# Run-in of a two-layer decoder kernel: one interleaved rounding order for the first weight parts and x pieces of both tiles

## The chip, the cores and the metric

The kernel runs on one core of a Trainium2 chip. The metric is the device time of one execution in microseconds; less is better. Before the change it is 1027.71 us, the median of three runs (1027.68 to 1027.79).

## What is computed

A residual stream x of 256 tokens by 1024 channels passes two layers, each a half-step SwiGLU FFN, a mixer (sliding-window attention in layer 0, gated DeltaNet in layer 1) and a second half-step FFN, then a last RMS norm. All is float32. The change is in the first FFN's first products alone:

```
def rms_norm(x, w):
    y = xf * lax.rsqrt(jnp.mean(xf * xf, axis=-1, keepdims=True) + NORM_EPS)
    return (y * w).astype(x.dtype)

def swiglu_ffn(h, w_gate_up, w_down):
    gate, up = jnp.split(h @ w_gate_up, 2, axis=-1)
    return (jax.nn.silu(gate) * up) @ w_down

h = h + 0.5 * swiglu_ffn(rms_norm(h, ffn1_norm[layer]), ffn1_w_gate_up[layer], ffn1_w_down[layer])
```

## The kernel before

**Products.** Every float32 operand is cut into two parts that TensorE takes at full rate: a high part (rounded by ScalarE, a Copy into fp32r) and a low part (the operand less its high part, by VectorE). `products` (L1691) then makes three matmuls of one: high by high, high by low, low by high. The x side is 128 tokens (a tile t of two), the weight side 512 columns.

**Weights.** Weights stream through a ring of four buffers of 128x2048, one "unit" each (w_raw, w_hi, w_lo). Unit u of the first FFN holds four 128-row slices (parts j = 0 to 3 of 512 columns) of one half kh of the 1024 input channels: units 0 and 1 are the first chunk's two halves, 2 and 3 the second chunk's, and so on. Units 0 to 2 are loaded, rounded and waited for by parts (`first_part` L508 on SP, `parts_hi` L732 on ScalarE, `parts_lo` L1153 on VectorE); from unit 3 on a unit is rounded whole (`split_hi` L725, `split_lo` L1147).

**x.** x is transposed by TensorE (`enter`, L1704) in quarters: a quarter n is a tile t and a half of the channels, four 128x128 transposes (pieces) into PSUM, in the order (t, half) = (0,0), (1,0), (0,1), (1,1). ScalarE evacuates each piece with the norm weight as scale into xT_hi (`enter_hi` L756), VectorE makes xT_lo from the same PSUM piece (`enter_lo` L1191). The factor of the RMS norm (rstd) is applied to results later. It needs squares of the whole x on ScalarE (`square` L749), then a root.

**The run-in.** SP issues the loads in order of use (from L557: x quarter, two weight parts, x quarter, two parts, x quarter, two parts of unit 1, x quarter, the rest; unit 2's parts; then unit 3 and on). ScalarE issues three small loads of norm weights and one of the convolution's weights (48 KB, L852), which is first used by a transpose at L1818, behind the first chunk. TensorE makes 14 warm-up transposes (L1835), the transpose of the norm rows (L1840), the first quarter of x and six more warm-ups. Then ScalarE (L858) and VectorE (L1329) take for each j one x piece of the first quarter and one weight part of unit 0, in turns, and only then the second and third quarters, unit 1's parts, the fourth quarter and unit 2's parts:

```
            for j in range(4):
                act.activation(xT_hi[:, j, 0:P], bank[FIRST_BANKS[j]][:, 0:P], ACT.Copy,
...
                act.wait_ge(part_loaded[0][j], 16)
...
                act.activation(w_hi[0][:, at], w_raw[0][:, at], ACT.Copy).then_inc(first_hi if j < 3 else hi_ready, 1)
            ffn(0)
```

TensorE's first chunk is `in_unit` (L1717), called for kh = 0 and 1: for tile 0 the four groups (one `products` call each) of parts 0 to 3, then for tile 1 the same. While kh = 0 and t = 0 it puts the remaining quarters' transposes behind groups 0, 2 and 3. So 16 groups, 48 matmuls:

```
                        if e == 0 and kh == 0 and t == 0 and j != 1:
                            enter(e, max(j, 1))
```

**Behind it.** The convolution transpose (L1818), then chunk 1 (`gate_chunk`, units 2 and 3; L1763 and L1765). Behind unit 2 stand `first_transposes` (L1771): the rstd rows and the transposes of the first chunk's result h. ScalarE meanwhile takes the squares, unit 3, the root, the silu of the first chunk (each of the last two behind a table load), units 4 and 5, and the high part of h; VectorE follows with the low parts (L1219, L1150, and L1227 for h). Chunk 2 on TensorE waits for h's low part (hT_lo_ready). All engines run their queues in order; every wait is a semaphore count.

## Time and profile before

| | |
|---|---|
| median of three runs | 1027.71 us (1027.68 to 1027.79) |
| profiled execution | 1027.81 us, its span 1026.1 us |
| TensorE busy (matmul) | 1015.8 us, 99% of the span |
| VectorE busy | 675.1 us, 66% |
| ScalarE busy | 569.1 us, 55% |
| GpSimd busy | 59.7 us, 6% |
| first product starts | 7.92 us |
| convolution transpose (first chunk done) | 20.65 us |

The span runs from the first to the last instruction of the profiled execution; starts are counted from its beginning. In the rows PE is TensorE's matmul, PEld its weight load, DVE VectorE, ACT ScalarE, SPq and ACTq the DMA issues of SP and ScalarE, and L and a number a line of the kernel. A row of the timeline can merge equal instructions that follow each other (x4): its second number is then the time from the first's start to the last's end. A matmul's duration includes its passage through the array, so matmuls overlap and their spacing is read from their starts.

### The profile page before, as it was taken

What the parts mean: (1) busy time and instruction counts of PE and PEld (TensorE: products, weight loads), DVE (VectorE), ACT (ScalarE), POOL (GpSimd) and SP (SyncE); (2) the same over time, 40 slices, a digit from 0 to 9 for tenths busy, and PEclk for the clock granted to TensorE, in tenths of its full rate; (3) what the DMA queues carried; (4) which work ended last, traced back from release to release, by engine and by line L of the source; (5) the groups of instructions that cost most, each with busy time, mean ns of one, the idle gap of its engine ahead of it and who ended that gap; (6) DMA issues with size and microseconds to landing.
All of it is one profiled execution on the core that took longest, in us unless ns stands there. A gap on an engine that the chain in (4) does not pass through costs nothing.

```text
span 1026.1 us, 15442 instructions
## 1 busy us (share of the span) xinstructions
PE 1015.8 (99%) x5784; PEld 880.5 (86%) x5784; DVE 675.1 (66%) x1005; ACT 569.1 (55%) x907; POOL 59.7 (6%) x120
## 2 busy tenths in 40 slices
PE   9999999999999999999999999999999999999997
PEld 7888888887888888888888888999999988888886
DVE  5766765576566776635766764688597666776733
ACT  7645543457465554536545543578567655554532
POOL 0000000110000000000000000404205100000000
PEclk9999999999999999999999999999999999999999
DMA  9665466343346555663666466343242347556521
GB/s 323 218 211 194 167 242 205 134 165 111 98 131 227 172 189 209 217 199 100 197 212 195 166 244 205 114 161 124 83 145 83 124 144 234 176 176 218 215 87 42
DMA packets 124308, 175.81 MB, mean 171 GB/s; under 512 B 7360, under 2 KB 97760, under 8 KB 124256
## 3 DMA queue, kind: packets, MB, share of 16 engines
q1 hardware_dynamic: 121552, 172.77, 50.6%
q10 hardware_dynamic: 2704, 2.33, 0.7%
q8 instruction: 34, 0.56, 0.2%
q14 instruction: 18, 0.15, 0.0%
HBM read 174.02 MB, written 1.06 MB: 171 GB/s over the span
## 4 chain that ended last, share of the span: by engine, by line
PE 97%; DVE 1%; ACT 1%; issue 0%; POOL 0%; ACTq 0%; POOLq 0%; DVEq 0%
PE bank L1763 29%; PE bank L1693 15%; PE bank L1695 15%; PE bank L1694 14%; PE bank L1765 14%; PE bank L2087 2%; PE bank L2081 2%; PE bank L1990 1%; PE bank L1714 1%; PE bank L1925 1%; PE bank L1956 1%; PE bank L1855 1%; PE bank L2187 0%; DVE x_sb L1187 0%; PE bank L1835 0%
## 5 line engine op out<-in xcount | busy, mean ns | idle before, releaser
L1763 PE MATMUL bank<-xT,w_hi 128*128 128x512 f32 x1280 | 444.9, 394 | 0.0
L1150 DVE TENSOR_TENSOR w_lo<-w_raw,w_hi 128x2048 fp32r<-128x2048 f32 x152 | 347.1, 2288 | 105.6 <-ACT w_hi L730 105.0
L730 ACT ACTIVATE w_hi<-w_raw 128x2048 fp32r<-128x2048 f32 x153 | 294.0, 1929 | 118.1 <-PE bank L1695 118.1
L1765 PE MATMUL bank<-xT,w_lo 128*128 128x256 f32 x1280 | 354.8, 277 | 0.0
L1763 PEld LDWEIGHTS bank<-xT,w_hi 128*128 128x128 f32 x1280 | 240.0, 188 | 55.9
L1765 PEld LDWEIGHTS bank<-xT,w_lo 128*128 128x128 f32 x1280 | 240.3, 188 | 0.1
L1693 PE MATMUL bank<-w_hi,hT_hi 128*128 128x512 f32 x352 | 137.5, 391 | 0.0
L1695 PE MATMUL bank<-w_hi,hT_lo 128*128 128x512 f32 x352 | 137.1, 389 | 0.0
L1694 PE MATMUL bank<-w_lo,hT_hi 128*128 128x512 f32 x352 | 137.0, 389 | 0.0
L796 ACT ACTIVATE silu_g<-bank 128x256 f32<-128x256 f32 x80 | 26.3, 382 | 175.4 <-PE bank L1765 175.4
L1237 DVE TENSOR_TENSOR silu_g<-bank,silu_g 128x256 f32<-128x256 f32 x80 | 30.2, 419 | 119.6 <-ACT silu_g L796 119.6
L1695 PEld LDWEIGHTS bank<-w_hi,hT_lo 128*128 128x128 f32 x352 | 66.1, 188 | 13.7
L1693 PEld LDWEIGHTS bank<-w_hi,hT_hi 128*128 128x128 f32 x352 | 66.1, 188 | 13.5
L1694 PEld LDWEIGHTS bank<-w_lo,hT_hi 128*128 128x128 f32 x352 | 66.1, 188 | 13.4
L1693 PE MATMUL bank<-w_hi,xT 128*128 128x512 f32 x144 | 59.9, 416 | 1.1 <-DVE w_lo L1343 0.7
L1695 PE MATMUL bank<-w_hi,xT 128*128 128x512 f32 x144 | 56.4, 392 | 0.0
L1694 PE MATMUL bank<-w_lo,xT 128*128 128x512 f32 x144 | 56.2, 390 | 0.0
L1693 PE MATMUL bank<-xT,w_hi 128*128 128x256 f32 x192 | 56.0, 292 | 0.0
L1695 PE MATMUL bank<-xT,w_lo 128*128 128x256 f32 x192 | 54.3, 283 | 0.0
L1694 PE MATMUL bank<-xT,w_hi 128*128 128x256 f32 x192 | 54.3, 283 | 0.0
L763 ACT ACTIVATE xT<-bank,norm_cols 128x128 fp32r<-128x128 f32 x92 | 26.2, 369 | 36.0 <-PE bank L1714 36.0
L1200 DVE SCALAR_TENSOR_TENSOR xT<-bank,norm_cols,xT 128x128 fp32r<-128x128 f32 x92 | 25.6, 343 | 24.6 <-ACT xT L763 24.6
(310 smaller groups left out, 1214.0 us busy)
## 6 DMA issues: line engine op xcount, KB each, us to landing
w_raw<-in_ffn_w_gate_up SPq DMA_DIRECT2D x170, 512.0 KB, 4.7
w_raw<-in_ffn_w_down SPq DMA_DIRECT2D x88, 512.0 KB, 4.2
w_raw<-in_gdn_w_in SPq DMA_DIRECT2D x32, 512.0 KB, 4.4
w_raw<-in_attn_w_in SPq DMA_DIRECT2D x12, 512.0 KB, 4.3
w_raw<-in_attn_w_out SPq DMA_DIRECT2D x8, 512.0 KB, 4.0
w_raw<-in_gdn_w_out SPq DMA_DIRECT2D x8, 512.0 KB, 3.9
w_raw<-in_ffn_w_gate_up SPq DMA_DIRECT2D x12, 256.0 KB, 5.5
x_sb<-in_x SPq DMA_DIRECT2D x4, 256.0 KB, 5.0
```

The costliest lines, as they stand in the source:

```text
L730: act.activation(w_hi[u0 % RING][:], w_raw[u0 % RING][:], ACT.Copy).then_inc(hi_ready, 1)
L763: z = act.activation(xT_hi[:, kt, t * P:(t + 1) * P], enter_bank(e, n, j), ACT.Copy, scale=norm_cols[:, norm_col(e, kt):norm_col(e, kt) + 1])
L796: z = act.activation(to[:, m, :], banks[2 * k + m][:, SEQ:2 * SEQ], ACT.Copy)
L1150: dve.tensor_tensor(w_lo[u0 % RING][:], w_raw[u0 % RING][:], w_hi[u0 % RING][:].bitcast(F32), ALU.subtract).then_inc(split_ready, 1)
L1200: z = dve.scalar_tensor_tensor(xT_lo[:, kt, t * P:(t + 1) * P], enter_bank(e, n, j), norm_cols[:, norm_col(e, kt):norm_col(e, kt) + 1], xT ...
L1237: z = dve.tensor_tensor(g[:, m, :], banks[m][:, 0:SEQ], g[:, m, :], ALU.add)
L1693: pe.matmul(out_ap, a[0], b[0], start=start, stop=False, **kw)
L1694: pe.matmul(out_ap, a[0], b[1], start=False, stop=False, **kw)
L1695: return pe.matmul(out_ap, a[1], b[0], start=False, stop=stop, **kw)
L1763: pe.matmul(banks[m][:], w[0], xT[:, kt, :, :].rearrange("p s n -> p (s n)"), start=(kt == 0), stop=False, skip_group_check=True)
L1765: z = pe.matmul(banks[m][:, 0:SEQ], w[1], xT_hi[:, kt, :], start=False, stop=(kt == KT - 1), skip_group_check=True)
L2081: z = pe.matmul(bank[b][:, h * P:(h + 1) * P], a(h), m(h), start=True, stop=True)
```

## The change

A list PIECES gives one order for the 12 operands of unit 0: four weight parts and the x pieces of both tiles' first halves. ScalarE and VectorE both follow it. Every x piece of the first two quarters has a bank or part of a bank of its own; quarter 2 goes to bank 1. The low part of every piece but three counts up first_split, for which TensorE waits by piece (PIECE_COUNT). TensorE's first chunk is the new `first_units`: in each unit the groups come in the order (t, j) = (0,0), (0,1), (1,0), (1,1), (0,2), (1,2), (0,3), (1,3), with the transposes of the other quarters behind the first, fifth and eighth group of unit 0. ScalarE and VectorE take the third quarter, two parts of unit 1, the fourth quarter, two parts, unit 2. The convolution rows' load goes from ScalarE's queue to SP's, behind unit 2's parts. The first FFN's `first_transposes` move from behind unit 2 to before the third part of unit 3. The first x quarter is transposed ahead of the norm rows, with 9 warm-ups before and 8 behind (14 and 6 before), in bank 6 instead of 5.

```diff
--- before.py
+++ after.py
@@ -276,7 +276,10 @@
             X_of = [[X[t], Lm[t]] for t in range(TT)]
 
         bank = [ctx.enter_context(nc.psum_tensor(f"bank{i}", [P, BANK], F32)) for i in range(8)]
-        FIRST_BANKS = [4, 0, 1, 3]
+        FIRST_BANKS = [[4, 0, 1, 5], [6, 7, 4, 0]]
+        PIECES = [("w", 0), (0, 0), (0, 1), ("w", 1), (0, 2), (1, 0), (1, 1), ("w", 2), (0, 3), (1, 2), ("w", 3), (1, 3)]
+        LAST_PIECES = [(0, 3), ("w", 3), (1, 3)]
+        PIECE_COUNT = {piece: 1 + n for n, piece in enumerate([q for q in PIECES if q not in LAST_PIECES])}
 
 
         ENTER_BANKS = {0: (4, 6), 1: (4, 2), 2: (4, 2), 3: (4, 6), 5: (4, 2)}
@@ -293,8 +296,10 @@
             t, half = quarters(e)[n]
             if e == E_GDN:
                 return bank[((4, 5), (6, 0), (4, 4), (5, 5))[n][j // 2]][:, j * P:(j + 1) * P]
-            if e == 0 and n == 0:
-                return bank[FIRST_BANKS[j]][:, 0:P]
+            if e == 0 and n < 2:
+                return bank[FIRST_BANKS[n][j]][:, 0:P]
+            if e == 0 and n == 2:
+                return bank[1][:, j * P:(j + 1) * P]
             return bank[ENTER_BANKS[e][t] + half][:, j * P:(j + 1) * P]
 
         def chunk_banks(f, j):
@@ -568,6 +573,7 @@
             first_part(1, 3)
             for j in range(4):
                 first_part(2, j)
+            sp.dma_start(conv_rows, gdn_conv_w[0].rearrange("j (t p) -> (j t) p", p=P)).then_inc(conv_loaded, 16)
             ffn(0, ffn1_w_gate_up[0], ffn1_w_down[0])
             for n, col in enumerate(ATT_COLS):
                 for kh in range(2):
@@ -729,9 +735,9 @@
                     act.wait_ge(unit_done, u0 - RING + 1 + 4 * i)
                 act.activation(w_hi[u0 % RING][:], w_raw[u0 % RING][:], ACT.Copy).then_inc(hi_ready, 1)
 
-            def parts_hi(u0):
-
-                for j in range(4):
+            def parts_hi(u0, js=range(4)):
+
+                for j in js:
                     act.wait_ge(part_loaded[u0][j], 16)
                     at = slice(j * BANK, (j + 1) * BANK)
                     act.activation(w_hi[u0][:, at], w_raw[u0][:, at], ACT.Copy).then_inc(
@@ -807,9 +813,10 @@
                 e, u = E_FFN[f], U_FFN[f]
                 if f == 0:
 
-                    enter_hi(e, range(1, 3))
-                    parts_hi(1)
+                    enter_hi(e, range(2, 3))
+                    parts_hi(1, range(2))
                     enter_hi(e, range(3, 4))
+                    parts_hi(1, range(2, 4))
                     parts_hi(2)
                 else:
                     enter_hi(e)
@@ -849,19 +856,22 @@
             for n, w in enumerate([ffn1_norm, mix_norm, ffn2_norm]):
                 act.dma_start(norm_rows[n * 2 * KT:(n + 1) * 2 * KT, :],
                               w.rearrange("l (t p) -> (l t) p", p=P)).then_inc(rows_loaded, 16)
-            act.dma_start(conv_rows,
-                          gdn_conv_w[0].rearrange("j (t p) -> (j t) p", p=P)).then_inc(conv_loaded, 16)
-            act.wait_ge(cols_psum, 1)
-            act.activation(norm_cols[:], bank[7][:, 0:NORM_ROWS], ACT.Copy).then_inc(cols_ready, 1)
-            act.wait_ge(cols_ready, 1)
-            act.wait_ge(xT_psum, 1)
-            for j in range(4):
-                act.activation(xT_hi[:, j, 0:P], bank[FIRST_BANKS[j]][:, 0:P], ACT.Copy,
-                               scale=norm_cols[:, norm_col(0, j):norm_col(0, j) + 1]).then_inc(
-                                   first_hi if j < 3 else xT_hi_ready, 1)
-                act.wait_ge(part_loaded[0][j], 16)
-                at = slice(j * BANK, (j + 1) * BANK)
-                act.activation(w_hi[0][:, at], w_raw[0][:, at], ACT.Copy).then_inc(first_hi if j < 3 else hi_ready, 1)
+            for piece in PIECES:
+                tile, j = piece
+                if tile == "w":
+                    act.wait_ge(part_loaded[0][j], 16)
+                    at = slice(j * BANK, (j + 1) * BANK)
+                    act.activation(w_hi[0][:, at], w_raw[0][:, at], ACT.Copy).then_inc(
+                        hi_ready if piece in LAST_PIECES else first_hi, 1)
+                else:
+                    act.wait_ge(xT_psum, tile + 1)
+                    act.activation(xT_hi[:, j, tile * P:(tile + 1) * P], enter_bank(0, tile, j), ACT.Copy,
+                                   scale=norm_cols[:, norm_col(0, j):norm_col(0, j) + 1]).then_inc(
+                                       xT_hi_ready if piece in LAST_PIECES else first_hi, 1)
+                if piece == ("w", 0):
+                    act.wait_ge(cols_psum, 1)
+                    act.activation(norm_cols[:], bank[7][:, 0:NORM_ROWS], ACT.Copy).then_inc(cols_ready, 1)
+                    act.wait_ge(cols_ready, 1)
             ffn(0)
 
 
@@ -1150,9 +1160,9 @@
                 dve.tensor_tensor(w_lo[u0 % RING][:], w_raw[u0 % RING][:], w_hi[u0 % RING][:].bitcast(F32),
                                   ALU.subtract).then_inc(split_ready, 1)
 
-            def parts_lo(u0):
-
-                for j in range(4):
+            def parts_lo(u0, js=range(4)):
+
+                for j in js:
                     at = slice(j * BANK, (j + 1) * BANK)
                     if j < 3:
                         dve.wait_ge(part_hi, 3 * (u0 - 1) + j + 1)
@@ -1277,10 +1287,10 @@
                     enter_lo(e, 3)
                     split_lo(PHASE_UNIT[e] + 2)
                 else:
-                    enter_lo(e, 1)
                     enter_lo(e, 2)
-                    parts_lo(1)
+                    parts_lo(1, range(2))
                     enter_lo(e, 3)
+                    parts_lo(1, range(2, 4))
                     parts_lo(2)
                 inverse_rms(TT * (e + 1))
 
@@ -1325,23 +1335,25 @@
                 after(dve.tensor_scalar(ang[:, 1], ang[:, 1], TWO_PI / 4, None, ALU.add))
                 dve.tensor_scalar(ang[:], ang[:], PI_BELOW, -PI_BELOW, ALU.min, ALU.max).then_inc(angle_ready, 1)
 
-            dve.wait_ge(cols_ready, 1)
-            for j in range(4):
-                at = slice(j * BANK, (j + 1) * BANK)
-                if j < 3:
-                    dve.wait_ge(first_hi, 2 * j + 1)
+            for piece in PIECES:
+                tile, j = piece
+                if piece in PIECE_COUNT:
+                    dve.wait_ge(first_hi, PIECE_COUNT[piece])
+                if tile == "w":
+                    if piece in LAST_PIECES:
+                        dve.wait_ge(hi_ready, 1)
+                    at = slice(j * BANK, (j + 1) * BANK)
+                    dve.tensor_tensor(w_lo[0][:, at], w_raw[0][:, at], w_hi[0][:, at].bitcast(F32),
+                                      ALU.subtract).then_inc(split_ready if piece in LAST_PIECES else first_split, 1)
                 else:
-                    dve.wait_ge(xT_hi_ready, 1)
-                z = dve.scalar_tensor_tensor(xT_lo[:, j, 0:P], bank[FIRST_BANKS[j]][:, 0:P],
+                    if piece in LAST_PIECES:
+                        dve.wait_ge(xT_hi_ready, tile + 1)
+                    dve.wait_ge(cols_ready, 1)
+                    at = slice(tile * P, (tile + 1) * P)
+                    dve.scalar_tensor_tensor(xT_lo[:, j, at], enter_bank(0, tile, j),
                                              norm_cols[:, norm_col(0, j):norm_col(0, j) + 1],
-                                             xT_hi[:, j, 0:P].bitcast(F32), ALU.mult, ALU.subtract)
-                if j < 3:
-                    dve.wait_ge(first_hi, 2 * j + 2)
-                else:
-                    z.then_inc(xT_lo_ready, 1)
-                    dve.wait_ge(hi_ready, 1)
-                dve.tensor_tensor(w_lo[0][:, at], w_raw[0][:, at], w_hi[0][:, at].bitcast(F32),
-                                  ALU.subtract).then_inc(first_split if j < 3 else split_ready, 1)
+                                             xT_hi[:, j, at].bitcast(F32), ALU.mult, ALU.subtract).then_inc(
+                                                 xT_lo_ready if piece in LAST_PIECES else first_split, 1)
             ffn(0, None)
 
 
@@ -1714,27 +1726,49 @@
                     z = pe.transpose(enter_bank(e, n, j), x_sb[:, t, kt * P:(kt + 1) * P], ident[:])
                 z.then_inc(xT_psum, 1)
 
+            def first_units(banks):
+
+                def tile_part(kh, t, j):
+                    return products(bank[banks[t]][:], x_of(4 * kh + j, t), ring(kh, slice(j * BANK, (j + 1) * BANK)),
+                                    start=(kh == 0 and j == 0), stop=(kh == 1 and j == 3))
+
+                for n, (t, j) in enumerate([(0, 0), (0, 1), (1, 0), (1, 1), (0, 2), (1, 2), (0, 3), (1, 3)]):
+                    for piece in ((t, j), ("w", j)):
+                        if piece in PIECE_COUNT:
+                            pe.wait_ge(first_split, PIECE_COUNT[piece])
+                        elif piece == ("w", 3):
+                            wait_split(pe, 0)
+                        else:
+                            pe.wait_ge(xT_lo_ready, t + 1)
+                    z = tile_part(0, t, j)
+                    if n == 0:
+                        pe.wait_ge(first_split, PIECE_COUNT[0, 1])
+                        enter(0, 1)
+                    elif n == 4:
+                        pe.wait_ge(first_split, PIECE_COUNT[0, 2])
+                        enter(0, 2)
+                    elif n == 7:
+                        z.then_inc(unit_done, 1)
+                        enter(0, 3)
+                for t, j in [(0, 0), (0, 1), (1, 0), (1, 1), (0, 2), (1, 2), (0, 3), (1, 3)]:
+                    pe.wait_ge(xT_lo_ready, 2 + t + 1)
+                    if j < 3:
+                        pe.wait_ge(part_split, j + 1)
+                    else:
+                        wait_split(pe, 1)
+                    z = tile_part(1, t, j)
+                z.then_inc(unit_done, 1)
+
             def in_unit(u0, i, kh, banks, e=None):
 
 
-                by_parts = u0 < FIRST and not looped(i)
-                if not by_parts:
-                    wait_split(pe, u0, i)
-                for t in range(TT):
-                    if e is not None and (e or kh or t):
+                wait_split(pe, u0, i)
+                for t in range(TT):
+                    if e is not None:
                         pe.wait_ge(xT_lo_ready, 4 * e + quarters(e).index((t, kh)) + 1)
                     for j in range(4):
-                        if by_parts and t == 0:
-                            if j < 3 and u0 == 0:
-                                pe.wait_ge(first_split, j + 1)
-                            elif j < 3:
-                                pe.wait_ge(part_split, 3 * (u0 - 1) + j + 1)
-                            else:
-                                wait_split(pe, u0)
                         z = products(bank[banks[t]][:], x_of(4 * kh + j, t), ring(u0, slice(j * BANK, (j + 1) * BANK)),
                                      start=(kh == 0 and j == 0), stop=(kh == 1 and j == 3))
-                        if e == 0 and kh == 0 and t == 0 and j != 1:
-                            enter(e, max(j, 1))
                     if t == TT - 1:
                         z.then_inc(unit_done, 1)
                     if e and kh == 0:
@@ -1753,6 +1787,8 @@
                     if not by_parts:
                         wait_split(pe, u0, i)
                     for q in range(4):
+                        if f == 0 and j == 1 and kh == 1 and q == 2 and not looped(i):
+                            first_transposes(f)
                         if by_parts and q < 3:
                             pe.wait_ge(part_split, 3 * (u0 - 1) + q + 1)
                         elif by_parts:
@@ -1765,7 +1801,7 @@
                             z = pe.matmul(banks[m][:, 0:SEQ], w[1], xT_hi[:, kt, :], start=False,
                                           stop=(kt == KT - 1), skip_group_check=True)
                     z.then_inc(unit_done, 1)
-                    if j == 1 and kh == 0 and not looped(i):
+                    if f and j == 1 and kh == 0 and not looped(i):
                         first_transposes(f)
 
             def first_transposes(f):
@@ -1811,8 +1847,11 @@
                 return hT_hi[:, at], hT_lo[:, at]
 
             def ffn(f, e_next):
-                for kh in range(2):
-                    in_unit(U_FFN[f] + kh, 0, kh, FIRST_CHUNK[f], E_FFN[f])
+                if f == 0:
+                    first_units(FIRST_CHUNK[f])
+                else:
+                    for kh in range(2):
+                        in_unit(U_FFN[f] + kh, 0, kh, FIRST_CHUNK[f], E_FFN[f])
                 if f == 0:
                     pe.wait_ge(conv_loaded, 16)
                     pe.transpose(bank[5][:, 0:CONV_ROWS], conv_rows,
@@ -1832,14 +1871,14 @@
             def warm(count):
 
                 for n in range(count):
-                    pe.transpose(bank[5][:, 0:P], ident[:], ident[:])
+                    pe.transpose(bank[6][:, 0:P], ident[:], ident[:])
 
             pe.wait_ge(ident_ready, 1)
-            warm(14)
+            warm(9)
+            enter(0, 0)
             pe.wait_ge(rows_loaded, 16 * 3)
             pe.transpose(bank[7][:, 0:NORM_ROWS], norm_rows, ident[0:NORM_ROWS, 0:NORM_ROWS]).then_inc(cols_psum, 1)
-            enter(0, 0)
-            warm(6)
+            warm(8)
             ffn(0, E_ATT)
 
 
```

## Rows read from the trace of the kernel before

**Rows 1.** The page: the chain that ended last, share of the span by engine.
```profile
PE 97%; DVE 1%; ACT 1%; issue 0%; POOL 0%; ACTq 0%; POOLq 0%; DVEq 0%
```

**Rows 2.** Timeline of TensorE (PE), first 21 us.
```profile
start us, us, engine line op out<-in xcount [idle before <-releaser]
1.60 3.25 PE L1835 MATMUL bank<-ident 128*128 128x128 f32 x14 [1.60 <-POOL ident L607]
...
5.95 1.26 PE L1835 MATMUL bank<-ident 128*128 128x128 f32 x6
...
7.92 0.50 PE L1693 MATMUL bank<-w_hi,xT 128*128 128x512 f32 x1 [0.71 <-DVE w_lo L1343]
...
8.73 0.60 PE L1714 MATMUL bank<-ident,x_sb 128*128 128x128 f32 x4
...
9.08 0.48 PE L1693 MATMUL bank<-w_hi,xT 128*128 128x512 f32 x1
...
11.96 0.65 PE L1714 MATMUL bank<-ident,x_sb 128*128 128x128 f32 x4
...
15.21 0.39 PE L1693 MATMUL bank<-w_hi,xT 128*128 128x512 f32 x1
...
20.65 0.25 PE L1818 MATMUL bank<-ident,h_row 96*128 96x96 f32 x1
```

**Rows 3.** Timeline of ScalarE (ACT) and VectorE (DVE), 6 to 18 us.
```profile
6.26 0.37 ACT L859 ACTIVATE xT<-bank,norm_cols 128x128 fp32r<-128x128 f32 x1 [0.90 <-PE bank L1714]
...
6.53 0.62 ACT L864 ACTIVATE w_hi<-w_raw 128x512 fp32r<-128x512 f32 x1
...
7.04 0.36 ACT L859 ACTIVATE xT<-bank,norm_cols 128x128 fp32r<-128x128 f32 x1
...
7.18 0.69 DVE L1343 TENSOR_TENSOR w_lo<-w_raw,w_hi 128x512 fp32r<-128x512 f32 x1
...
7.79 0.35 DVE L1335 SCALAR_TENSOR_TENSOR xT<-bank,norm_cols,xT 128x128 fp32r<-128x128 f32 x1
...
8.57 0.63 ACT L864 ACTIVATE w_hi<-w_raw 128x512 fp32r<-128x512 f32 x1 [0.40 <-DMA w_raw<-in_ffn_w_gate_up]
...
11.43 1.14 ACT L763 ACTIVATE xT<-bank,norm_cols 128x128 fp32r<-128x128 f32 x4 [0.42 <-PE bank L1714]
...
12.60 1.12 DVE L1200 SCALAR_TENSOR_TENSOR xT<-bank,norm_cols,xT 128x128 fp32r<-128x128 f32 x4 [0.43 <-ACT xT L763]
...
17.61 1.09 ACT L750 ACTIVATE y_sb<-x_sb 128x1024 f32<-128x1024 f32 x1
```

**Rows 4.** Timeline of SP's issues, and what the norm rows' landing released.
```profile
0.82 0.40 SPq L544 DMA_DIRECT2D x_sb<-in_x  x1
...
1.27 1.31 SPq L511 DMA_DIRECT2D w_raw<-in_ffn_w_gate_up  x2
...
4.77 0.18 PEld L1840 LDWEIGHTS bank<-ident,h_row 48*128 48x128 f32 x1 [0.33 <-DMA h_row<-in_ffn_norm]
```

**Rows 5.** DMA view of single issues (x at 0.82; parts 0, 1): KB, us to landing.
```profile
x_sb<-in_x SPq DMA_DIRECT2D x1, 256.0 KB, 2.9
...
w_raw<-in_ffn_w_gate_up SPq DMA_DIRECT2D x1, 256.0 KB, 3.9
...
w_raw<-in_ffn_w_gate_up SPq DMA_DIRECT2D x1, 256.0 KB, 4.6
```

**Rows 6.** Timeline behind the run-in, 19 to 33 us.
```profile
19.69 1.94 ACT L730 ACTIVATE w_hi<-w_raw 128x2048 fp32r<-128x2048 f32 x1
...
27.13 4.49 DVE L1150 TENSOR_TENSOR w_lo<-w_raw,w_hi 128x2048 fp32r<-128x2048 f32 x2 [1.33 <-ACT w_hi L730]
...
31.55 0.68 DVE L1227 TENSOR_TENSOR hT_lo<-bank,hT_hi 128x512 fp32r<-128x512 f32 x1
...
32.62 0.39 PE L1763 MATMUL bank<-xT,w_hi 128*128 128x512 f32 x1
```

**Rows 7.** Warm-up transposes by line: ns min/median/max, first and last start us.
```profile
L1835 PE MATMUL bank<-ident x20: 273/421/473, 1.6 to 6.9; 128*128 128x128 f32 x20
```

**Rows 8.** Windows, 0 to 7 us: busy us of each engine, PEclk behind POOL.
```profile
core 0: us, PE busy (x) PEld busy (x) DVE busy (x) ACT busy (x) POOL busy (x), PEclk, DMA share, GB/s
0.00:7.00 7.00, 5.40 (x25) 4.96 (x25) 0.26 (x1) 2.23 (x4) 0.70 (x6) 1.00 0.63 184
```

## Prediction

> **What bounds the kernel now.** The page first: the chain that ended last is 97% TensorE [rows 1], so the time is the length of TensorE's work plus the few places where it waits. The timeline of the first 45 us, TensorE's rows alone, shows those places in the run-in [rows 2]: 14 warm-up transposes from 1.60, six more from 5.95 to 7.2, then nothing until the first product at 7.92, released by VectorE's first weight part. The first FFN chunk is 16 groups of three products (48 matmuls) with 12 transposes of x between them, and it ends at 20.65, where the convolution transpose starts. The prices of TensorE's steps come from these rows: a group that follows a wait lasts 8.73 - 7.92 = 0.81 us, a group in a steady stream (20.65 - 15.21) / 8 = 0.68, four transposes delay the next group by 9.08 - 8.73 = 0.35 and their result is whole after 0.60. Without any wait the 16 groups and 12 transposes would take 16 x 0.68 + 0.13 + 3 x 0.35 = 12.06 us; they take 20.65 - 7.92 = 12.73. From 15.21 on, where unit 1 begins, TensorE never waits. So what can be won is the start at 7.92 and about 0.6 us of gaps, and whatever the new order loses counts in full, because everything behind 20.65 is TensorE's chain.
>
> The rows of ScalarE and VectorE [rows 3] give the other prices. ScalarE: a weight part (128x512) is 0.62 long and the next operation starts 7.04 - 6.53 = 0.51 later; an x piece (128x128) is 0.36 and the next starts 0.27 later. VectorE: a part 0.69, next after 7.79 - 7.18 = 0.61; an x piece 0.34, next after (1.12 - 0.34) / 3 = 0.26. An operation released by the other engine starts about 0.04 behind its end; TensorE starts 0.05 behind VectorE (7.18 + 0.69 to 7.92). Arrivals [rows 4, 5]: the first x quarter lands at 0.82 + 2.9 = 3.72, the first weight part at 1.27 + 3.9 = 5.17, the second, whose issue ends the 1.31 us from 1.27 and so begins near 2.0, at 2.0 + 4.6 = 6.6, the norm rows by 4.77; the third part landed at 8.57 [rows 3], the last x quarter at 11.96 [rows 2].
>
> **The change, step by step.** *Start.* 9 warm-ups at the pace of the six (1.26 / 6 = 0.21) end near 3.5; the x quarter follows at its landing, 3.75, and is whole by 4.9; norm rows and 8 warm-ups follow, done near 6.7. ScalarE now rounds part 0 first, 5.20 to 5.82, then copies the norm columns (5.72), then x piece 0 at 5.99 to 6.36, x piece 1 at 6.26, part 1 at its landing, 6.60 to 7.22. VectorE: part 0 at 5.86, x piece 0 at 6.47 to 6.82, x piece 1 to 7.08, part 1 at 7.26 to 7.95. First product: 6.82 + 0.05 = 6.87, against 7.92: 1.05 us won.
>
> *Unit 0.* Group (0,0) ends 7.68; the four transposes of tile 1 are whole at 8.28; group (0,1) meanwhile, to about 8.8. Group (1,0) needs the first of those pieces through ScalarE (8.32 to 8.68) and VectorE (8.72 to 9.07): it starts at 9.12, a wait of 0.3. It ends 9.93, (1,1) 10.61, (0,2) 11.29: part 2 (landed 8.57, ScalarE 8.86, VectorE 9.52 to 10.21) is ready. Transposes of the third quarter at 11.29, whole at 11.89. The last three groups have their operands (VectorE's last piece ends near 11.6) and end at 11.64 + 2.14 = 13.78; the fourth quarter's transposes end unit 0 at 14.13. Before, TensorE was at this point at 15.21: it is now 1.08 ahead.
>
> *Unit 1* gives it back. ScalarE and VectorE have run out of work by 11.6 and wait for the third quarter: ScalarE 11.93 to 13.07 (four pieces, 1.14), VectorE 13.11 to 14.23, and only then does VectorE take weight part 0 of unit 1, ready at 14.84. TensorE waits from 14.13 to 14.89 and restarts: that group lasts 0.81. Group (0,1) ends 16.38. Group (1,0) needs the fourth quarter: transposes whole at 14.38, ScalarE (after two parts, idle from 14.0) 14.42 to 15.56, VectorE 15.60 to 16.72. TensorE starts it at 16.77, a wait of 0.39, and goes on with 0.81 + 5 x 0.68: the chunk ends at 20.98. Before, tile 1's groups of unit 0 stood between these operands and their use; now they have been spent. Sum to here: +0.33.
>
> *Behind it.* ScalarE's squares started at 17.61; now its queue holds four x pieces and six parts from 14.42: 14.42 + 1.0 + 6 x 0.52 = 18.54, later by 0.93. That lateness runs on through table loads, first chunk and splits of units 4 and 5 to VectorE, which follows ScalarE there (idle 1.33 before the two L1150) and reaches the low part of h at 31.55 [rows 6]. TensorE needs it at 32.62 for chunk 2: slack 32.62 - 32.23 = 0.39. TensorE is 0.33 later, VectorE 0.93: 33.16 + 0.05 against 32.95 is a wait of 0.26, with the restart some 0.35. The first transposes of h, moved from behind unit 2 into the middle of unit 3 (some 2.8 us of products later), cost the same wherever they stand, and give h's rows, which come from the late first chunk, more time; their result finds VectorE still at its two splits, so the move costs nothing at 31.55 and saves nothing there. Sum: 0.33 + 0.35 = +0.68.
>
> *Edits costed at nothing.* Three warm-ups fewer, and another bank for them: TensorE idles before the first product in any case. Banks of their own for pieces: no wait is added beyond those counted. The extra waits on TensorE, ScalarE and VectorE are met when reached, save the ones above; if each took some hundredths the sum would grow by up to 0.2. The convolution rows' load moves from ScalarE's queue (fourth there, beside the first parts) behind 16 transfers on SP. It puts one issue of 0.6 us ahead of unit 3's loads, which ScalarE needed only at 19.69 [rows 6] and now needs 0.93 later; the rows themselves are needed at 20.98, nearly ten us after their issue (16 transfers at 1.31 / 2 from 0.82), against landing times of 2.9 to 4.6 [rows 5]. In its old place it took bytes beside part 1, which lands 6.6 - 5.17 = 1.43 behind part 0: 48 KB against 256 KB are at most 48/256 of that, 0.27, and at least nothing. The sum above passes little of it on, since it hangs on TensorE's own transposes; I take -0.08, nearer to nothing, and the forecast is +0.6. The Trainium skill (DMA: Bandwidth & Descriptors, section "Issuing engines are not separate DMA queues") says that transfers issued by different engines interleave on the same 16 DMA engines. By that rule the load costs the same bytes wherever it is issued, and only its place in time can help; if that place is worth nothing, the sum stays +0.68 instead of +0.60. Part 1's late landing fits the rule without proving it.
>
> The profiled execution took 1027.81 us around a span of 1026.1, the median of three is 1027.71; I put the 0.6 on the median: 1028.3.
>
> **Rivals.** *A: the lead is kept.* If unit 1's operands came in time, the end would move by -1.05 to -1.3 (the old gaps too), half of it if only one of the two waits comes: 1026.5 to 1027.6. For: VectorE's work for 16 pieces and 8 parts is 16 x 0.26 + 8 x 0.61 = 9.0 us in a stretch of 14. Against: each quarter goes through three engines whole, 0.60 + 1.14 + 1.12 us before the first use, and its transposes stand later in the groups' order than before. Chance 0.22.
>
> *B: slower by over 0.2%, the array's pace.* The granted clock is recorded as 1.00 over the first 7 us [rows 8], but transposes come every 0.21 us from 5.95 (1.26 / 6) and every 0.11 at 8.73 ((0.60 - 0.27) / 3): the early ones go at the pace of the lower level, 1.2 GHz, the later ones at 2.4, and the shortest warm-up (273 ns, median 421) is already one of the faster kind, after almost unbroken work since 1.60 [rows 7]. The first product would now stand at 6.87, just there, behind three fewer warm-ups and two gaps of some 0.2. If the pace rose only after another stretch as long as the first (1.60 to 6.9, 5.3 us), half of that, 2.6, would be lost, some 0.2 of it in the wait at 9.12: 1028.3 + 2.4 = 1030.7. It decides from 1.5 us lost. The Trainium skill (TensorE: Matmul & The Clock Gate, Part 1) has the throttled state as the default that activity releases, and warns that recorded clock events can be unreliable; the pace of these rows agrees with both. Chance 0.05.
>
> *C: the early start fails.* If norm rows or part 0 come late behind the new order, or piece 0 of x (third in ScalarE's queue now) waits, the first product stays near 7.9 and the waits of unit 1 remain, since they hang on TensorE's own transposes: +0.6 + 1.0, 1029.3. Chance 0.06.
>
> **Numbers.** Forecast case 0.67 (+0.0 to +1.1: no lateness at chunk 2, or every added wait and both restarts dearer), A 0.22, B 0.05, C 0.06. The range runs from half of A to the top of the forecast case: 1027.1 to 1029.0, leaving out the lower half of A, B and C, 0.2 together. What a measurement can tell here is 0.2%, 2.06 us; all but B lie inside. Faster 0.02, same 0.93, slower 0.05.
>
> **What would show it.** Right: first product at 6.8 to 7.0 and at full pace (second one 0.34 behind the first), a gap near 9, waits before the first and third group of unit 1, convolution transpose near 21.0, squares near 18.5, a wait before chunk 2's first product. Wrong: no gap at 14 to 15 and the convolution transpose at 19.9 or earlier (A), matmuls 0.43 apart (512 columns at 1.2 GHz) behind the first product (B), first product after 7.5 (C).

## The result, and the profile after

The changed kernel takes 1030.12 us (median of 20, 1028.62 to 1032.00), the kernel before 1027.74 beside it (20, 1027.41 to 1029.74). The medians are 2.4 us apart (slower), where +0.6 was forecast; the ratio on record is 1.0021, 95% interval 1.0014 to 1.0027. The ratios given here are those on record, not quotients of the medians (1.0023 here), so they can differ from them in the fourth place. The executions fall in groups: six at 1028.62 to 1028.95, five at 1029.86 to 1030.14, six at 1030.48 to 1030.81, three at 1031.90 to 1032.00. The profiled one took 1030.54. The lines of the page for it:

```profile
span 1028.8 us, 15460 instructions
...
PE 1017.2 (99%) x5781; PEld 880.0 (86%) x5781; DVE 675.3 (66%) x1005; ACT 569.3 (55%) x907; POOL 59.8 (6%) x120
...
PE 95%; ACT 2%; DVE 2%; issue 1%; DMA 0%; SPq 0%; ACTq 0%; DVEq 0%
```

The last line answers to [rows 1]. TensorE lost two points of the chain to the others: followed in time, the chain now lies on ScalarE and VectorE from 14.56 to chunk 2's first product at 33.35 (x pieces, weight parts, squares, root and silu, the splits, the low part of h). The timeline of the changed kernel shows where (start, length, instruction, idle before it and its releaser):

```profile
7.00 0.50 PE L1705 MATMUL bank<-w_hi,xT 128*128 128x512 f32 x1 [0.90 <-DVE xT L1353]
...
9.24 0.50 PE L1705 MATMUL bank<-w_hi,xT 128*128 128x512 f32 x1
...
15.10 0.47 PE L1705 MATMUL bank<-w_hi,xT 128*128 128x512 f32 x1 [0.57 <-DVE w_lo L1171]
...
16.92 0.50 PE L1705 MATMUL bank<-w_hi,xT 128*128 128x512 f32 x1 [0.20 <-DVE xT L1210]
...
18.70 1.06 ACT L756 ACTIVATE y_sb<-x_sb 128x1024 f32<-128x1024 f32 x1
...
21.14 0.25 PE L1857 MATMUL bank<-ident,h_row 96*128 96x96 f32 x1
...
32.62 0.68 DVE L1237 TENSOR_TENSOR hT_lo<-bank,hT_hi 128x512 fp32r<-128x512 f32 x1
...
33.35 0.50 PE L1799 MATMUL bank<-xT,w_hi 128*128 128x512 f32 x1
```

Against [rows 2, 3, 6]: first product 7.92 to 7.00, convolution transpose 20.65 to 21.14, squares 17.61 to 18.70, h's low part 31.55 to 32.62, chunk 2's first product 32.62 to 33.35. So the changed kernel is 0.73 late at chunk 2's first product. At 134 us, where the first FFN's gate and up part ends, it is 2.73 late, and 2.7 at the end. The other 2.0 us arise between 33 and 134 us, where no engine's order was touched and TensorE shows no wait. The windows of TensorE alone, 40 to 100 us (us, busy and matmuls in brackets, granted clock, DMA share, GB/s), first the kernel before, then the changed one:

```profile
40.00:100.00 60.00, 60.00 (x348) 1.00 0.63 201
```
```profile
40.00:100.00 60.00, 60.00 (x341) 1.00 0.59 190
```

Both are 100% busy at a clock of 1.00, with the same instructions. One starts 348 matmuls, the other 341. The work of a unit is 16 pairs, each one matmul of 512 columns and one of 256. Start by start, a unit takes 5.547 us before and 5.65 to 5.66 after, in every unit from chunk 2 to the end of the first FFN's gate and up part. The spacings form a pattern that repeats: over two pairs in 0.693 us in the first rhythm, over three pairs in 1.060 us in the second. These are called the fast and the slow rhythm below. The stretch of 18 units costs 18 x 0.106 = 1.9 us, and 0.1 is the restart behind the wait at 33.35. The other three FFNs run in the fast rhythm behind chunk 2 in both profiles.

Where did the slow rhythm begin in this profile? Not at the wait. Six pairs take 28.88 - 26.80 = 2.08 us ahead of h's transposes, and 32.70 - 30.58 = 2.12 behind them, still ahead of the wait:

```profile
26.80 0.39 PE L1799 MATMUL bank<-xT,w_hi 128*128 128x512 f32 x1
...
28.88 0.39 PE L1799 MATMUL bank<-xT,w_hi 128*128 128x512 f32 x1
...
29.80 0.60 PE L1818 MATMUL bank<-ident,h_row 128*128 128x128 f32 x4
...
30.58 0.40 PE L1799 MATMUL bank<-xT,w_hi 128*128 128x512 f32 x1
...
32.70 0.40 PE L1799 MATMUL bank<-xT,w_hi 128*128 128x512 f32 x1
```

So there are two candidates, h's transposes and the wait ahead of chunk 2. The experiments take them apart.

### The profile page after: what moved, and what is told of

Same layout as the page of the kernel before. It is cut to its first block, busy times and chain, and to the rows that moved or that the text cites. A ratio compares the mean times of both kernels' runs of the same rounds, so it can differ in the third digit from the quotient of the medians.

```text
span 1028.8 us, 15460 instructions
## 1 busy us (share of the span) xinstructions
PE 1017.2 (99%) x5781; PEld 880.0 (86%) x5781; DVE 675.3 (66%) x1005; ACT 569.3 (55%) x907; POOL 59.8 (6%) x120
## 4 chain that ended last, share of the span: by engine, by line
PE 95%; ACT 2%; DVE 2%; issue 1%; DMA 0%; SPq 0%; ACTq 0%; DVEq 0%
PE bank L1799 28%; PE bank L1705 14%; PE bank L1707 14%; PE bank L1706 14%; PE bank L1801 14%; PE bank L2126 2%; PE bank L2120 2%; PE bank L2029 1%; PE bank L1726 1%; PE bank L1964 1%; PE bank L1995 1%; PE bank L1894 1%; DVE w_lo L1160 0%; DVE x_sb L1197 0%; PE bank L2226 0%
## 5 line engine op out<-in xcount | busy, mean ns | idle before, releaser
L809 ACT ACTIVATE hT_hi<-h_row 128x512 f32 (+1 forms) x40 | 25.3, 633 | 29.0 <-DVE h_row L1259 29.0
```

The lines of the kernel that those rows point to most:

```text
L809: act.activation(hT_hi[:, bass.ds((j + 2 * i) * BANK, BANK)], h_row[j % 2][:].rearrange("p m n -> p (m n)"), ACT.Copy).then_inc(hT_hi_read ...
```

## Experiments: what changes the rhythm

The experiments ran in four groups, each on one chip beside the kernel before; "of n" counts executions. The kernel before had 33, 32, 27 and 21 executions in the four groups, medians 1027.79, 1027.69, 1027.74, 1027.73, and 11 of these 113 above 1029.2.

**h's transposes back in their place**, in the changed kernel:

```diff
-                        if f == 0 and j == 1 and kh == 1 and q == 2 and not looped(i):
-                            first_transposes(f)
...
-                    if f and j == 1 and kh == 0 and not looped(i):
+                    if j == 1 and kh == 0 and not looped(i):
                         first_transposes(f)
```

> The changed kernel with one part undone: the transposes of the first chunk's h stand behind unit 2 again instead of in the middle of unit 3. Theory 1 (two rhythms: the 512/256-column pairs of the first FFN run at 5.55 or 5.65 us per unit of 16 pairs, and the transposes' place decides which one the following 18 units take): units from unit 3 on at 5.547, chunk 2 starts 0.6 to 0.8 behind the kernel before, the time 1028.3 to 1028.8. Rival (the late run-in, its shifted loads or its wait ahead of chunk 2 slow the units): units stay at 5.65 and the time near 1030.3. In both the wait for h's rows behind unit 2 is under 0.2 us.

Median 1030.44 (of 11), ratio 1.0023 (1.0014 to 1.0032); four executions at 1028.2 to 1028.65, five at 1030.4 to 1030.8, two above 1032. The profiled one (1028.53) has all 18 units at 5.547. The place doesn't decide alone, and neither does the late run-in by itself: one kernel runs both ways.

**That move alone, in the kernel before**: the same lines the other way round.

> The kernel before with this part of the change alone: the transposes of h moved from behind unit 2 into the middle of unit 3. Theory 1 (the place decides the rhythm): the units behind it at 5.65 and the time near 1029.7, though the run-in is the old one. Rival (the run-in's lateness slows the units): units at 5.547 and 1027.7, as before.

Median 1027.85, ratio 0.9999 (0.9990 to 1.0008); three of 11 above 1029.3. The move by itself costs nothing in most executions. Its profile caught one of the three (1030.35): units at 5.65, and the early products 0.36 to 0.59 apart until 9.7 us. (Here and with the transposes cut in two, further down, the move in the kernel before has six of 22 executions above 1029.2, the kernel before 11 of 113. Whether the move makes late executions more frequent can't be told from so few.)

**Quarters of x transposed earlier**, in the changed kernel:

```diff
-                    elif n == 4:
+                    elif n == 3:
                         pe.wait_ge(first_split, PIECE_COUNT[0, 2])
                         enter(0, 2)
+                    elif n == 5:
+                        enter(0, 3)
                     elif n == 7:
                         z.then_inc(unit_done, 1)
-                        enter(0, 3)
```

> The changed kernel with the third quarter's transposes of x behind the fourth group of unit 0 instead of the fifth, and the fourth quarter's behind the sixth instead of the eighth. By the account of the run-in (quarters reach ScalarE too late) the waits at unit 1's first and third group fall from 0.57 and 0.20 idle to under 0.25 each, and the convolution transpose starts at 20.1 to 20.3 instead of 21.14; ScalarE's squares start near 17.6 instead of 18.70. If the waits hang on something else (arrivals, weight parts) it stays at 20.9 or later. The time is then the one that the rhythm gives: 1027.3 in the fast one, 1029.3 in the slow one.

> Both edits: quarters' transposes earlier and h's transposes behind unit 2 again. Convolution transpose at 20.1 to 20.3; behind unit 2 h's rows are waited for by up to 0.6 us, since TensorE is there 0.5 earlier than in the kernel before. If the place decides the rhythm: units at 5.547 and 1027.3 to 1027.8, at or below the kernel before; if not, up to 1029.5.

The timeline of the first one:

```profile
17.47 1.09 ACT L756 ACTIVATE y_sb<-x_sb 128x1024 f32<-128x1024 f32 x1
...
20.10 0.25 PE L1858 MATMUL bank<-ident,h_row 96*128 96x96 f32 x1
```

The convolution transpose moves from 21.14 to 20.10 and the squares from 18.70 to 17.47, and TensorE's waits at unit 1's first and third group are gone from the profile: the account of unit 1's waits is right. Of the 1.04 us, 0.25 is an earlier first product (6.75, not 7.00) and 0.79 a shorter chunk. The time doesn't follow: 1029.39 (ratio 1.0012, 1.0003 to 1.0021), one execution at 1027.42 and ten at 1029.2 to 1029.7. With h's transposes back in their place it is 1029.60 (1.0020, 1.0011 to 1.0029), none below 1029.0 and four of 11 at 1031.0 to 1031.3; 1029.5 at most was expected if the place doesn't decide. Both profiles show a tiny wait ahead of chunk 2 (0.02 to 0.04 us beyond the usual spacing of the pairs), the fast rhythm ahead of it and the slow one behind it. That suggested the next four.

**The wait ahead of chunk 2 taken away, added, and the changed kernel again.** Taken away (in the changed kernel, and in the one with earlier quarters):

```diff
                 split_lo(u + 4)
-                split_lo(u + 5)
+                if f:
+                    split_lo(u + 5)
...
                                   ALU.subtract).then_inc(hT_lo_ready, 1)
+                if f == 0:
+                    split_lo(U_FFN[f] + 5)
                 dve.wait_ge(rows_ready, ROWS_FFN[f])
```

Added, in the kernel before:

```diff
             def first_hT_lo(f):
 
+                if f == 0:
+                    dve.tensor_scalar(y_sb[:, 0, :], x_sb[:, 0, :], 1.0, None, ALU.mult)
                 dve.wait_ge(hT_hi_ready, NCH * f + 1)
```

> The changed kernel with the wait ahead of chunk 2 taken away: VectorE makes h's low part before unit 5's instead of behind it. Theory (a wait right ahead of chunk 2's first product picks the rhythm of all the pairs behind it anew in every execution; without one they keep the rhythm they have, mostly the fast one): no idle ahead of chunk 2, most executions in the fast rhythm, median near 1028.3. Rival 1 (the rhythm is drawn somewhere in the run-in, or by the place of h's transposes): the time falls only by the wait itself, 0.35, and most executions stay slow, median near 1030.

> The kernel before with such a wait added: one extra VectorE operation over 128x1024 ahead of h's low part, some 0.6 to 1.1 us, against 0.34 of slack. Its result goes to a scratch tile. Theory: the wait itself costs 0.3 to 0.9 and most executions change to the slow rhythm, median 1029.5 to 1030.7. Rival (the rhythm is drawn elsewhere): the wait alone, 1028.1 to 1028.7.

> Earlier quarters' transposes of x and no wait ahead of chunk 2. Theory: the fast rhythm in most executions and the run-in's gain kept, median 1027.0 to 1027.4, below the kernel before. Rival: 1029.2.

> The changed kernel unaltered, beside the first one on the same chip. Theory: executions fall in groups near 1028.7, 1030.0 to 1030.8 and 1032, most of them in the middle one; its profile, whichever group it falls in, has units 4 to 21 of the first FFN all at 5.547 or all at 5.65 us.

The changed kernel again: 1030.53 (of 10), one at 1028.72, nine at 1030.3 to 1030.8. Its timeline at the wait, the pairs' first matmuls alone:

```profile
31.51 0.39 PE L1799 MATMUL bank<-xT,w_hi 128*128 128x512 f32 x1
...
31.86 0.39 PE L1799 MATMUL bank<-xT,w_hi 128*128 128x512 f32 x1
...
32.20 0.39 PE L1799 MATMUL bank<-xT,w_hi 128*128 128x512 f32 x1
...
32.55 0.39 PE L1799 MATMUL bank<-xT,w_hi 128*128 128x512 f32 x1
...
32.90 0.39 PE L1799 MATMUL bank<-xT,w_hi 128*128 128x512 f32 x1
...
33.42 0.19 PEld L1799 LDWEIGHTS bank<-xT,w_hi 128*128 128x128 f32 x1 [0.33 <-DVE hT_lo L1237]
...
33.88 0.40 PE L1799 MATMUL bank<-xT,w_hi 128*128 128x512 f32 x1
...
34.24 0.40 PE L1799 MATMUL bank<-xT,w_hi 128*128 128x512 f32 x1
...
34.59 0.40 PE L1799 MATMUL bank<-xT,w_hi 128*128 128x512 f32 x1
...
34.94 0.40 PE L1799 MATMUL bank<-xT,w_hi 128*128 128x512 f32 x1
...
35.30 0.40 PE L1799 MATMUL bank<-xT,w_hi 128*128 128x512 f32 x1
```

Four pairs take 32.90 - 31.51 = 1.39 us ahead of the wait and 35.30 - 33.88 = 1.42 behind it; from the unrounded starts, a unit's worth is 5.55 and 5.65. Here the rhythm changes at the wait. In the first profile of the same kernel it had changed at h's transposes.

The wait added to the kernel before shows as 0.16 us at TensorE's weight load, and at its matmul as hardly anything. The pair's start comes 0.35 behind the one ahead of it, as usual, and only the next comes late, at 0.46 instead of 0.35:

```profile
31.27 0.69 DVE L1227 TENSOR_SCALAR y_sb<-x_sb 128x1024 f32<-128x1024 f32 x1
...
31.87 0.68 DVE L1229 TENSOR_TENSOR hT_lo<-bank,hT_hi 128x512 fp32r<-128x512 f32 x1
...
32.26 0.39 PE L1765 MATMUL bank<-xT,w_hi 128*128 128x512 f32 x1
...
32.61 0.19 PEld L1765 LDWEIGHTS bank<-xT,w_hi 128*128 128x128 f32 x1 [0.16 <-DVE hT_lo L1229]
...
32.61 0.50 PE L1765 MATMUL bank<-xT,w_hi 128*128 128x512 f32 x1
...
33.07 0.40 PE L1765 MATMUL bank<-xT,w_hi 128*128 128x512 f32 x1
```

The median rose to 1029.67 (ratio 1.0013, 1.0004 to 1.0022): four executions at 1027.5 to 1028.15, seven at 1029.4 to 1029.9, while of the kernel before's 32 beside it five are above 1029.2. A wait whose own cost is some 0.1 costs 2 us in seven executions of 11. Its profile (1029.77) goes from 5.547 ahead of the wait to 5.65 behind it.

Taken away from the changed kernel, the median is 1029.50 (1.0014, 1.0005 to 1.0023): five executions at 1027.8 to 1028.5, three at 1029.5 to 1029.7, three at 1030.1 to 1030.4. That lies between the two theories. The profiled execution has no wait for h and keeps 5.547 from unit 3's last two parts to the end of the stretch:

```profile
31.25 0.69 DVE L1238 TENSOR_TENSOR hT_lo<-bank,hT_hi 128x512 fp32r<-128x512 f32 x1 [0.74 <-ACT hT_hi L792]
...
31.86 2.28 DVE L1160 TENSOR_TENSOR w_lo<-w_raw,w_hi 128x2048 fp32r<-128x2048 f32 x1
```

With earlier quarters as well it is 1027.42 (0.9998, 0.9989 to 1.0007), seven of 11 at 1026.97 to 1027.47 and four near 1029. A wait is a cause of the rhythm's change, but not the only source of late executions.

**Is it any interruption, and is it this FFN?** h's transposes cut in two (`first_rows` are the two of rstd, `first_h` the four of h). In the changed kernel, the main lines; the kernel before gets the same two calls together with the move out of unit 2:

```diff
+                        if f == 0 and j == 1 and kh == 1 and q == 1 and not looped(i):
+                            first_rows(f)
                         if f == 0 and j == 1 and kh == 1 and q == 2 and not looped(i):
-                            first_transposes(f)
+                            first_h(f)
```

And a wait in the second FFN alone, in the kernel before:

```diff
                 dve.wait_ge(hT_hi_ready, NCH * f + 1)
+                if f == 1:
+                    for n in range(3):
+                        after(dve.tensor_tensor(hT_lo[:, 0:BANK], bank[4][:], hT_hi[:, 0:BANK].bitcast(F32),
+                                                ALU.subtract))
```

> The kernel before with h's transposes moved into unit 3 and cut in two: the two of rstd before its second part, the four of h before its third. No wait is added. Theory (ten profiles so far: unit 2 mostly runs slow, 5.64, and every interruption of the pairs by transposes changes the rhythm to the other one; so does a wait): two changes bring it back to slow, units from chunk 2 on at 5.65 in most executions, median 1029.4 to 1030.0, against 1027.85 for the same move in one piece. Rival 1 (only a wait draws the rhythm anew, transposes lead to the fast one): 1027.8 to 1028.1.

> The changed kernel with h's transposes cut in two in the same way. Theory of changes: unit 2 slow, then fast, slow, and fast again at the wait ahead of chunk 2: most executions fast, median 1028.4 to 1029. Rival 1 (the wait leads to the slow rhythm, whatever stands ahead): 1030.3 to 1030.7 as for the changed kernel.

> The kernel before with a wait of 0.4 to 1 us ahead of chunk 2 of the second FFN alone: VectorE makes h's low part four times there. If a wait changes the rhythm anywhere: the second FFN's units from chunk 2 on at 5.65, the first FFN's at 5.547, median 1030 to 1030.9. If the effect belongs to the first FFN alone: the wait itself, 1028.1 to 1028.8.

Cut in two in the kernel before: 1027.88 (1.0003, 0.9994 to 1.0012). In the changed kernel: 1030.47 (1.0022, 1.0013 to 1.0031). Both miss what the theory of changes gave; that every interruption changes the rhythm has fallen. In both profiles the four transposes of h changed it, once to the fast rhythm and once to the slow one, while the rhythm ahead of the two of rstd still stands behind them; only four pairs lie between the two, too few to rest much on.

Over all 16 profiles, before and after included, the first FFN shows this:

- In 15 of 16, TensorE came to the transposes of h without a wait, and in all 15 the rhythm changed there. Unit 2, ahead of them, ran slow in 12 of the 16 and fast in four: the changed kernel's first profile, the changed kernel with the transposes cut in two, the move alone, and the filled run-in further down. Those four are slow behind the transposes.
- A wait stands ahead of chunk 2 in nine profiles (one of them in the second FFN). Behind it the units ran slow in eight. Six of the eight were fast ahead of it; the other two, the changed kernel's first profile and the one with transposes cut in two, were slow already and stayed so. The ninth, with h's transposes back in their place, went from slow to fast.
- The second to fourth FFN give 48 more stretches, of which one alone has an edit (the next experiment). In all 48, unit 2 runs slow and the rhythm turns fast at the transposes of h behind it. 47 stay fast; the 48th is the one with a wait.

The wait in the second FFN (the pair's start comes 0.7 us late): 1030.50 (1.0023, 1.0014 to 1.0032), with three executions at 1028.5 to 1029.1 and one at 1032.84. The windows of its profile, TensorE alone, first FFN and second:

```profile
40.00:100.00 60.00, 60.00 (x349) 1.00 0.62 201
320.00:380.00 60.00, 60.00 (x341) 1.00 0.58 190
```

The first FFN keeps its rhythm and the second, fast behind chunk 2 in the other 15 profiles, takes the slow one behind the wait. It is no property of the first FFN.

## Experiments: the array's pace in the run-in

**No warm-ups**, in the changed kernel:

```diff
-            warm(9)
             enter(0, 0)
...
-            warm(8)
             ffn(0, E_ATT)
```

> The changed kernel without its 17 warm-up transposes. If TensorE's pace rises only after work (transposes 0.21 apart become 0.11 apart, at 5.2 in one profile and 9.7 in another), the first products here run 0.42 apart for some us in every execution: unit 1 ends 1.5 to 3 us later than in the changed kernel and the time is 1030.3 to 1032 in its fastest executions, against 1028.6. If the late rises have nothing to do with the work ahead of them, the fastest executions stay at 1028.7.

1031.95 (of 5, 1031.07 to 1032.38), ratio 1.0035 (1.0021 to 1.0048). TensorE's timeline:

```profile
6.64 0.80 PE L1705 MATMUL bank<-w_hi,xT 128*128 128x512 f32 x1 [1.64 <-DVE xT L1353]
7.24 0.63 PE L1706 MATMUL bank<-w_lo,xT 128*128 128x512 f32 x1
7.66 0.63 PE L1707 MATMUL bank<-w_hi,xT 128*128 128x512 f32 x1
...
22.50 0.25 PE L1857 MATMUL bank<-ident,h_row 96*128 96x96 f32 x1
```

Products come 0.42 to 0.43 apart (512 columns at 1.2 GHz) until 11 us, and the chunk ends 1.36 later than in the changed kernel, a little less than expected. Its first product stands 0.36 earlier, so the chunk itself is 1.72 longer. The pace does depend on work ahead. The same thing happened by itself in one profile of the kernel with earlier quarters and no wait (1028.96 us; its units behind h's transposes at 5.547):

```profile
7.41 0.79 PE L1708 MATMUL bank<-w_hi,xT 128*128 128x512 f32 x1
8.00 0.63 PE L1709 MATMUL bank<-w_lo,xT 128*128 128x512 f32 x1
8.43 0.63 PE L1710 MATMUL bank<-w_hi,xT 128*128 128x512 f32 x1
8.85 1.05 PE L1729 MATMUL bank<-ident,x_sb 128*128 128x128 f32 x4
```

and not in another of the same kernel (1026.84 us):

```profile
6.34 0.50 PE L1708 MATMUL bank<-w_hi,xT 128*128 128x512 f32 x1 [0.47 <-DVE xT L1356]
6.68 0.40 PE L1709 MATMUL bank<-w_lo,xT 128*128 128x512 f32 x1
6.91 0.39 PE L1710 MATMUL bank<-w_hi,xT 128*128 128x512 f32 x1
7.24 0.63 PE L1729 MATMUL bank<-ident,x_sb 128*128 128x128 f32 x4
```

In the first the convolution transpose comes at 21.75, in the second at 19.68: of the 2.07, 1.07 is the first product's later start (norm rows and first part landed later), and 1.0 the pace. Over the profiles with warm-ups the spacing halves between 4 and 10 us, at no fixed time. With the run-in of the kernel before it does so ahead of the first product in four profiles of five.

The windows view seems to contradict this. Without warm-ups it has a granted clock of 1.00 over the first 11 us, while the products come at the pace of 1.2 GHz:

```profile
0.00:11.00 11.00, 5.71 (x17) 4.36 (x18) 3.42 (x9) 5.23 (x13) 0.70 (x6) 1.00 0.79 237
```

**Is it the idle stretch ahead of the norm rows?** In the two profiles with the latest rise (9.66 and 10.04) TensorE's starts are 0.8 us apart ahead of the norm rows' transpose. The idle time is filled:

```diff
             enter(0, 0)
+            warm(3)
...
-            warm(8)
+            warm(6)
```

> Earlier quarters and no wait ahead of chunk 2, with three warm-ups between the x quarter and the norm rows and six instead of eight behind them, so that TensorE has no idle 0.5 to 0.8 us there. Theory (the slow group near 1029 of this kernel is a late rise of TensorE's pace, 9.6 us in the profile, 1.6 us lost, and the idle stretch ahead of the norm rows favours it): the group shrinks to 0 to 2 of 11 executions, median 1027.2 to 1027.5, the rise in the profile at 5 to 7.5. Rival (the rise falls where it falls, whatever stands there): 3 to 5 of 11 near 1028.9 again.

> The kernel with earlier quarters and no wait ahead of chunk 2 once more, beside the first one on the same chip: groups at 1027.0 to 1027.5 (two thirds) and near 1029; median 1027.4. It gives the base for the other, and tells whether the median lies below the kernel before a second time.

Filled: 1027.37 (0.9999, 0.9990 to 1.0008), four of 11 at 1028.9 to 1029.2. Unfilled: 1027.27 (0.9996, 0.9987 to 1.0005), two of 11 above 1028. Filling the stretch did not shrink the group, as the rival said; with 11 executions each, a smaller effect can't be told. The profile of the filled one (1028.92) had the full pace from 6.01, ahead of its first product, and the slow rhythm: its group near 1029 is, at least in part, the rhythm. How often each of the two occurs can't be separated by times alone.

The kernel with earlier quarters and no wait is the best of all tried: medians 1027.42 and 1027.27 against 1027.69 and 1027.73, 16 of its 22 executions below 1027.5 against 8 of the kernel before's 53. By its intervals it is not told from the kernel before.

## Why the prediction was wrong

- **First product 6.87**: 7.00 in the profile. Right, and its spacing was at the full pace.
- **Unit 0's gap and unit 1's two waits** (9.12, 14.89, 16.77): 9.24, 15.10, 16.92. Right to 0.2, and their cause is shown by the earlier quarters, which took both waits away.
- **Chunk ends 20.98, squares 18.54, wait ahead of chunk 2**: 21.14, 18.70, and a wait of 0.30 (0.65 between the pairs' starts instead of 0.35) where 0.26 was forecast. The forecast had chunk 2's first product 0.59 late, and 0.68 with the restart behind it; measured were 0.73 and 0.84. The executions at 1028.62 to 1028.95 fit this sum, but no profile of the changed kernel fell among them.
- **Convolution rows**: no wait for them or for unit 3's loads; -0.08 can't be told from nothing.
- **Where it failed**: the step "slack 32.62 - 32.23 = 0.39", which ends in "a wait of 0.26, with the restart some 0.35". The wait was priced at its own length, and the spacing of all pairs behind it was put at nothing, under "whatever the new order loses counts in full, because everything behind 20.65 is TensorE's chain". What stood behind it was the slow rhythm for 18 units, 1.9 us. In the second profile of the changed kernel the wait brought it. In the first, unit 2 ran fast, the transposes of h turned it slow, and the wait left it so; there "the move costs nothing" is in doubt as well, though with the transposes in their old place the median is the same (1030.44). The rows of before held the sign of it: unit 2 took 5.65 and the units behind h's transposes 5.547, with the same instructions and no wait.
- **Rival B** looked at the right place, the early pace, and gave 2.4 us at a chance of 0.05. What was seen costs 1.0 by the pair of profiles and 1.7 without warm-ups, and is found in profiles of altered kernels. For the changed kernel, the groups at 1029.86 to 1030.14 and at 1031.90 to 1032.00 lie some 1.3 above the two others and would fit it, but no profile fell in them: this is not shown. The first product's start varies too (6.42 to 7.05 in five profiles with this run-in and its warm-ups), so the slow rhythm behind an early start could account for part of the group at 1030.0. Its reading of [rows 8] was wrong: the granted clock was not recorded as 1.00 over the first 7 us, the first record there begins at 6.84, just where the pace doubles. A and C did not happen.
- **The range**: its top, 1029.0, is not the top of the forecast case, which is 1027.71 + 1.1 = 1028.8. The measured 1030.12 lies outside either.

The median of 1030.12 lies between the groups. Six of the 20 executions stand where the run-in's loss alone puts them. The nine at 1030.48 and above fit that loss plus 1.9 for the slow rhythm, and both profiles of the changed kernel lie among these times. The five near 1030.0 are open: the late pace, or the slow rhythm behind an early start. The rhythm's part is shown by the profiles, by the wait taken away and by the wait added; the pace's part in the changed kernel is argued from the times. What in TensorE makes two rhythms, why unit 2 starts fast in some executions, and why four transposes change the rhythm stays open.

## What to carry to other kernels

On an engine that is the bound, compare the spacing of equal instructions over the whole span, not only its waits: a lag that grows evenly where nothing was edited is a change of rhythm. A wait that itself costs a tenth of a microsecond, ahead of a long stretch of mixed matmul lengths, was followed here by a loss of 2 us in most executions, so the slack at the head of such a stretch is worth more than the same slack elsewhere. Profile a changed kernel more than once: its first two profiles had the same time and the same slow stretch, and it began in different places. When work is moved earlier in a run-in, the effect of the warm-ups may not be there yet in each execution. And a clock column of 1.00 ahead of the first clock record is not a measurement; the spacing of equal matmuls is.

## What the runs showed of the hardware

- A stream of pairs of 512 and 256 columns has two stable spacings at the same granted clock of 1.00, 5.547 and 5.65 us per 16 pairs, 1.9% apart, kept for 100 us once taken.
- Four 128-column transposes between such pairs changed the spacing in 15 of 15 profiles of the first FFN and in all 48 stretches of the other FFNs. A wait ahead of them led from the fast to the slow spacing in six of six.
- The spacing of TensorE's first transposes and products halves at a time that differs between executions, from 4.4 to 10 us into the span with warm-ups; without them it was 11.2. In all 16 traces the first clock record, at full speed, begins between the last start at the low pace and the first at the full one.
